# A two-layer decoder step on one Trainium2 core: the first loads are cut and reordered, and the last residual update is regrouped over three engines

## The reference, cut to what matters

```python
def trunk_layer(x, l, ...):
    h = rmsnorm(x, g_mix_pre[l])
    qa, ka, va, qi, ki, wi, qb, kb, vb, gb = project_mixers(h, w_in[l], pos)
    a = mixer_a(qa, ka, va, qi, ki, wi)            # indexer picks keys, sparse attention
    b, S = retention_mixer(qb, kb, vb, gb, s0, g_ret[l])
    x = x + rmsnorm(concat(a, b) @ w_out[l], g_mix_post[l])
    f = jnp.square(jax.nn.relu(rmsnorm(x, g_ffn_pre[l]) @ w_up[l])) @ w_down[l]
    return x + rmsnorm(f, g_ffn_post[l])

def rmsnorm(x, g):
    return x * lax.rsqrt(jnp.mean(x * x, axis=-1) + EPS) * g
```

## Time and profile before

| | us |
|---|---|
| median of 3 runs (1651.63 to 1654.96) | 1653.7 |
| the profiled execution, its own time | 1654.42 |
| its span, first to last instruction | 1652.6 |
| TensorE busy | 1580.8 |
| VectorE busy | 831.6 |
| ScalarE busy | 432.5 |
| GpSimd busy | 420.8 |

### The profile page before, as it was taken

The page is one execution under the profiler, slowest core; times in us unless marked ns, Lnnn a source line. Parts: engine busy times, 40 slices in busy tenths (PEclk is TensorE's granted clock), DMA queues, the critical chain, the costliest instruction groups (busy, mean ns, idle before and its releaser), DMA issues.

```text
span 1652.6 us, 19575 instructions
## 1 busy us (share of the span) xinstructions
PE 1580.8 (96%) x6986; PEld 1101.5 (67%) x6986; DVE 831.6 (50%) x1761; ACT 432.5 (26%) x975; POOL 420.8 (25%) x332
## 2 busy tenths in 40 slices
PE   7999899999999999999989998999999999999995
PEld 4344344478888888888843433445888888888884
DVE  4498556684743002332566984577646420133335
ACT  4312244314422002210142212443244310032100
POOL 0000000113363433353420000010226433343451
PEclk9999999999999999999999999999999999999998
DMA  6135401121422122312123252101233312222211
GB/s 203 63 127 167 146 20 52 53 78 55 153 102 103 72 82 102 103 51 102 63 94 102 77 202 105 52 1 54 81 103 127 105 74 103 102 80 100 77 51 52
DMA packets 52498, 150.26 MB, mean 91 GB/s; under 512 B 8331, under 2 KB 29331, under 8 KB 39091
## 3 DMA queue, kind: packets, MB, share of 16 engines
q1 hardware_dynamic: 44770, 140.65, 24.3%
q10 hardware_dynamic: 7632, 8.36, 1.5%
HBM read 139.79 MB, written 9.02 MB: 90 GB/s over the span
## 4 chain that ended last, share of the span: by engine, by line
PE 76%; DVE 16%; ACT 3%; issue 2%; DMA 2%; SPq 1%; ACTq 0%; DVEq 0%; POOL 0%; POOLq 0%
PE ps L1028 42%; PE ps L690 17%; PE ps L966 7%; DVE arena L1604 1%; DVE x_feat L1753 1%; DVE top L1602 1%; DVE arena L1643 1%; PE ps L694 1%; PE ps L828 1%; ACT arena L1182 1%; DVE s_sb L1751 1%; PE ps L815 1%; PE ps L838 1%; PE ps L649 1%; PE ps L924 1%
## 5 line engine op out<-in xcount | busy, mean ns | idle before, releaser
L690 PE MATMUL ps<-wring,h_feat 128*128 128x512 f32 (+1 forms) x960 | 438.6, 596 | 4.2 <-ACT arena L1182 2.8
L690 PEld LDWEIGHTS ps<-wring,h_feat 128*128 128x128 f32 x960 | 173.3, 193 | 192.7 <-issue 181.2
L1028 PE MATMUL ps<-arena,wring 128*128 128x256 f32 (+1 forms) x1280 | 285.8, 382 | 0.3 <-DVE arena L1832 0.3
L1028 PEld LDWEIGHTS ps<-arena,wring 128*128 128x128 f32 x1280 | 243.1, 190 | 37.7 <-DVE arena L1832 1.1
L1028 PE MATMUL ps<-h_feat,wring 128*128 128x256 f32 (+1 forms) x768 | 176.8, 382 | 2.5 <-DVE arena L1832 2.5
L2086 POOL TENSOR_TENSOR wring<-wring,arena 128x512 f32<-128x512 f32 (+1 forms) x48 | 78.8, 1641 | 341.2 <-PE ps L1028 321.6
L1028 PEld LDWEIGHTS ps<-h_feat,wring 128*128 128x128 f32 x768 | 145.8, 190 | 24.8 <-DVE arena L1832 3.3
L1028 PE MATMUL ps<-mix,wring 128*128 128x256 f32 (+1 forms) x512 | 123.6, 391 | 3.9 <-DVE s_sb L1806 3.9
L1028 PE MATMUL ps<-arena 128*128 128x264 f32 x512 | 119.2, 386 | 0.0
L966 PE MATMUL ps<-mix,wring 128*128 128x256 f32 (+1 forms) x512 | 115.0, 383 | 0.8 <-ACT mix L1242 0.8
L1028 PEld LDWEIGHTS ps<-mix,wring 128*128 128x128 f32 x512 | 99.4, 194 | 20.9 <-DVE s_sb L1806 4.8
(11 more groups left out here) (212 smaller groups left out, 1800.8 us busy)
## 6 DMA issues: line engine op xcount, KB each, us to landing
wring<-in_w_all SPq DMA_DIRECT2D x108, 1024.0 KB, 5.0
arena<-in_cache_k SPq DMA_DIRECT2D x32, 256.0 KB, 5.3
arena<-in_cache_v SPq DMA_DIRECT2D x32, 256.0 KB, 4.3
wring<-in_w_idx SPq DMA_DIRECT2D x4, 648.0 KB, 5.6
x_feat<-in_x SPq DMA_DIRECT2D x4, 520.0 KB, 6.4
o_k_out<-arena ACTq DMA_DIRECT2D x2, 1024.0 KB
o_v_out<-arena ACTq DMA_DIRECT2D x2, 1024.0 KB
arena<-in_state SPq DMA_DIRECT2D x2, 1024.0 KB, 4.9
```

Source lines behind the costliest of these rows:

```text
L690: last = mm(ps[:, proj_bank(n), 0:width], h_feat[:, k, token_cols(t)], wt, start=(k == 0), stop=(k == KD - 1))
L1028: last = mm(out, a[:, j, :], b, start=(opens(n) and j == 0), stop=(j == nk - 1), skip_group_check=True)
```

## The change

The x loads now come in pieces of 1, 1, 2, 2, 2 chunks and the first weights in pieces of 1, 1, 2, 4 chunks, issued alternately; `pg` comes after them. The squares of half 1, k = 4 and 6, in the last norm of both layers, are written by ScalarE to free slots of `p1s`; GpSimd no longer adds them, and TensorE multiplies them by the same matrix as `ssum`, into the same bank. In layer 1, for half 1, VectorE makes only the scaled product, in place in `osb`, with no wait between; TensorE has copied `x_feat` into eight banks by a product with the identity, adds the scaled `osb` by another, and ScalarE copies each bank to `x_feat`. The store of half 1 is cut into 4, 2 and 2 chunks.

```diff
+X_CUTS = (0, 1, 2, 4, 6, 8)
+W_CUTS = (0, 1, 2, 4, 8)
...
+def square_direct(norm, h, k):
+    return (norm, h) == (4, 1) and k in (4, 6)
...
+        def y_bank(k):
+            return ps[:, [n for n in range(8) if n != stat_bank(4)][k] if k < KD - 1 else stat_bank(4), 0:span(1)]
+        def direct_square(k):
+            return p1_at(LAST - 3 + (k == 6))
...
+            for n in range(len(X_CUTS) - 1):
+                k = slice(X_CUTS[n], X_CUTS[n + 1])
+                sp.dma_start(x_feat[:, k, :], x[:, k, :]).then_inc(x_in[n], 16)
+                if n < len(W_CUTS) - 1:
+                    u, cols = W_CUTS[n] // 4, slice(W_CUTS[n] % 4 * W_IDX, (W_CUTS[n] % 4 + W_CUTS[n + 1] - W_CUTS[n]) * W_IDX)
+                    sp.dma_start(wring[u][:, cols], w_idx[0, u, :, cols]).then_inc(first_w[n], 16)
             sp.dma_start(pg[:], pages).then_inc(pages_in, 16)
-            for k in range(0, KD, 2):
-                sp.dma_start(x_feat[:, k:k + 2, :], x[:, k:k + 2, :]).then_inc(x_in[k // 2], 16)
-                if k in (0, 4):
-                    u = k // 4
-                    sp.dma_start(wring[u][:, 0:4 * W_IDX], w_idx[0, u]).then_inc(first_w[u], 16)
...
-            for h in range(2):
-                for k in range(0, KD, 4):
-                    sp.wait_ge(x_ready, past(x_ready) + 2 * KD + h * KD + k + 4)
-                    sp.dma_start(y[:, k:k + 4, HALVES[h]], x_feat[:, k:k + 4, HALVES[h]]).then_inc(y_out, 16)
...
+            for k0, k1 in ((0, 4), (4, 6), (6, KD)):
+                sp.wait_ge(y_read, k1)
+                sp.dma_start(y[:, k0:k1, HALVES[1]], x_feat[:, k0:k1, HALVES[1]]).then_inc(y_out, 16)
...
-                mm(ps[:, stat_bank(4), 0:span(1)], ones[:], ssum[:, HALVES[1]], start=True, stop=True).then_inc(stat_mm, 1)
+                bank = ps[:, stat_bank(4), 0:span(1)]
+                mm(bank, ones[:], ssum[:, HALVES[1]], start=True, stop=False)
+                for k in (4, 6):
+                    pe.wait_ge(sq_ready, layer * PER_LAYER["sq_ready"] + square_number(layer, 4, 1, k)[0])
+                    last = mm(bank, ones[:], direct_square(k), start=False, stop=(k == 6))
+                last.then_inc(stat_mm, 1)
...
                     last_stats(l)
+                    pe.wait_ge(c12_ready, past(c12_ready) + LAST + 1)
+                    for k in range(KD):
+                        if k == KD - 1:
+                            pe.wait_ge(std_ready, counts[stat_mm.num])
+                        mm(y_bank(k), idn[:], x_feat[:, k, HALVES[1]], start=True, stop=False)
+                    for k in range(KD):
+                        pe.wait_ge(last_upd, k + 1)
+                        mm(y_bank(k), idn[:], osb[:, k, HALVES[1]], start=False, stop=True).then_inc(y_mm, 1)
...
                     deviation(4, 1)
+                    for k in range(KD):
+                        act.wait_ge(y_mm, k + 1)
+                        nc.scalar.activation(x_feat[:, k, HALVES[1]], y_bank(k), ACT.Copy).then_inc(y_read, 1)
...
-                for k in range(KD):
+                for k in range(KD if l == DEPTH - 1 else 0):
+                    o = osb[:, k, HALVES[1]]
+                    v.scalar_tensor_tensor(o, o, gcol[:, 2, k:k + 1], rstd_post[:, HALVES[1]], ALU.mult, ALU.mult).then_inc(last_upd, 1)
+                for k in range(KD if l < DEPTH - 1 else 0):
                     update(2, 1, k)
...
+                if square_direct(norm, h, k):
+                    return
```

More of the change, by code:

```diff
@@ L88, in head_steps, with cut_of @@
     return [(k, done(n, k)) for k in range(KD) if done(n, k + 1) > done(n, k)]
+def cut_of(cuts, k):
+    return max(n for n, c in enumerate(cuts[:-1]) if c <= k)
 def product_items():
@@ L205 @@
     c12_ready=24, ft_ready=64, c11_dve=4, dn_ready=16, knew_done=8, gain_ready=5, osq_ready=5,
-    pads_ready=1, sq_used=56, s_ready=96, kidx_in=256, gains_in=32, state_in=16, out_ki=32, out_k=32, out_v=32,
+    pads_ready=1, sq_used=54, s_ready=96, kidx_in=256, gains_in=32, state_in=16, out_ki=32, out_k=32, out_v=32,
     out_r=48, bounce=64, bounce_o=16, w_slot0=208, w_slot1=208, w_slot2=224, w_slot3=224, c_slot0=128, c_slot1=128,
@@ L226, in square_number @@
     n = order.index((norm, h, k)) + 1
-    return n, sum(1 for s in order[0:n] if not square_first(*s))
+    return n, sum(1 for s in order[0:n] if not square_first(*s) and not square_direct(*s))
 def counter():
@@ L354, in build @@
         const_in = sem("const_in"); zeroed = sem("zeroed"); y_out = sem("y_out")
-        x_in = [sem(f"x_in{i}") for i in range(KD // 2)]
+        x_in = [sem(f"x_in{i}") for i in range(len(X_CUTS) - 1)]
         gfirst_in = sem("gfirst_in")
-        first_w = [sem(f"first_w{i}") for i in range(2)]
+        first_w = [sem(f"first_w{i}") for i in range(len(W_CUTS) - 1)]
         pages_in = sem("pages_in")
@@ L365, in build @@
         state_in = sem("state_in")
+        last_upd = sem("last_upd")
+        y_mm = sem("y_mm")
+        y_read = sem("y_read")
         sq_ready = sem("sq_ready")
@@ L604, in _ @@
                     unit(u)
-            for h in range(2):
-                for k in range(0, KD, 4):
-                    sp.wait_ge(x_ready, past(x_ready) + 2 * KD + h * KD + k + 4)
-                    sp.dma_start(y[:, k:k + 4, HALVES[h]], x_feat[:, k:k + 4, HALVES[h]]).then_inc(y_out, 16)
-            sp.wait_ge(y_out, 64)
+            for k in range(0, KD, 4):
+                sp.wait_ge(x_ready, past(x_ready) + 2 * KD + k + 4)
+                sp.dma_start(y[:, k:k + 4, HALVES[0]], x_feat[:, k:k + 4, HALVES[0]]).then_inc(y_out, 16)
+            for k0, k1 in ((0, 4), (4, 6), (6, KD)):
+                sp.wait_ge(y_read, k1)
+                sp.dma_start(y[:, k0:k1, HALVES[1]], x_feat[:, k0:k1, HALVES[1]]).then_inc(y_out, 16)
+            sp.wait_ge(y_out, 80)
         @block.tensor
@@ L631, in last_stats @@
             def last_stats(layer):
-                pe.wait_ge(sq_used, layer * PER_LAYER["sq_used"] + max(square_number(layer, 4, 1, k)[1] for k in range(KD)))
+                pe.wait_ge(sq_used, layer * PER_LAYER["sq_used"] + max(square_number(layer, 4, 1, k)[1] for k in range(KD) if not square_direct(4, 1, k)))
                 pe.wait_ge(std_ready, counts[stat_mm.num])
-                mm(ps[:, stat_bank(4), 0:span(1)], ones[:], ssum[:, HALVES[1]], start=True, stop=True).then_inc(stat_mm, 1)
+                bank = ps[:, stat_bank(4), 0:span(1)]
[4 more added lines that the diff above has]
+                last.then_inc(stat_mm, 1)
                 up(stat_mm)
@@ L653, in first_chunk @@
                 for k in range(KD):
-                    if k % 4 == 0:
-                        pe.wait_ge(first_w[k // 4], 16)
+                    if k in W_CUTS:
+                        pe.wait_ge(first_w[cut_of(W_CUTS, k)], 16)
                     pe.wait_ge(first_h, k + 1)
@@ L1087, in _ @@
             for k in range(KD):
-                act.wait_ge(x_in[k // 2], 16)
+                act.wait_ge(x_in[cut_of(X_CUTS, k)], 16)
                 nc.scalar.activation(h_feat[:, k, :], x_feat[:, k, :], ACT.Copy, scale=gfirst[:, k:k + 1]).then_inc(first_h, 1)
@@ L1109, in square @@
                     dst = ssum[:, HALVES[h]]
+                elif square_direct(norm, h, k):
+                    dst = direct_square(k)
                 else:
@@ L2041, in _ @@
                 inverse(1, rstd_post)
-                for k in range(KD):
+                for k in range(KD if l == DEPTH - 1 else 0):
+                    o = osb[:, k, HALVES[1]]
+                    v.scalar_tensor_tensor(o, o, gcol[:, 2, k:k + 1], rstd_post[:, HALVES[1]], ALU.mult, ALU.mult).then_inc(last_upd, 1)
+                for k in range(KD if l < DEPTH - 1 else 0):
                     update(2, 1, k)
-                    if k == 2 and l < DEPTH - 1:
+                    if k == 2:
                         now[0] = l + 1
```

## The result

The changed kernel took 1639.61 us (median of 4 executions, 1635.28 to 1641.46), against 1652.66 for the kernel before, run beside it (4 executions, 1651.55 to 1654.96). The ratio on record is 0.9915, 95% interval 0.9892 to 0.9939 (the two medians alone give 0.9921): faster, by about 13 us or 0.8%. The profiled execution took 1641.46, the longest of its four, with a span of 1639.7 against 1652.6. So profile against profile the change is worth 12.9 us, where the prediction had 11.4.

A forecast was written before the change was run, and what follows sets the result against it. TensorE carries 76% of the chain, VectorE 16%, so gains come only where TensorE stands still. Start 6.5, end of layer 0 0.1, end 4.8 sum to 11.4: 1654.42 to 1643.0, less 0.7 gives 1642.3 us; range 1640.0 to 1647.0.

The forecast's parts named there:

- the end of layer 0: Where layer 0 ends: two additions leave GpSimd, VectorE gains 1.0 us, more products cost 0.9; net 0.1 gained.
- the base: Whole kernel: profiled execution 1654.42 us, with the median of the runs shown 0.7 lower.
- First loads: At the start: smaller pieces let TensorE start at 4.8 us instead of 6.85 and end the first projection at 26.0.
- the start term: Start to second projection: first bank taken 6.1 to 6.9 us earlier, counted as 6.5; second projection at 28.5.
- the bound of 7.0: At the start: the gain cannot pass 31.31 - 24.3 = 7.0 us, since TensorE's first bank is complete at 24.3.
- Constants: At the start: `pg` last holds the weight units until 21.3 us, so the last constant lands at 21.8 to 22.9.
- `wring2` too late: At the second projection: each us these weights land after 28.5 costs one; a loss at 39.9, 26.5 expected; chance 0.02.
- the whole rest moves forward together: After the start: all later loads wait on work done, so everything shifts equally, with 0 gained in layer 0's body.
- the middle loses: Rival, end of layer 0: remaining GpSimd additions slide under other VectorE instructions, products cost 0.9 us; time 1643.3; chance 0.08.
- Statistics at the end: At the end: the last statistics product starts 1.5 us earlier without GpSimd's wait, plus 0.4 less; gain 1.9.
- The last update and the store: At the end: TensorE sets the pace, last copy ends at 1644.8 us instead of 1649.19, store at 1647.8; 2.9 gained.
- The clock rival: Last 10 us: TensorE's clock at half; time 1649.6 us with all records slow, 1646.0 with half; chance 0.15.

The follow-up runs named there:

- r_after_again: The changed kernel run again unedited (also called the repetition): 1638.51 us, ratio 0.9915 to the kernel before.
- e1: The kernel before with only the new start (first loads in cut pieces, `pg` behind them), nothing at the end: 1644.61 us, ratio 0.9955.
- e2: The kernel before with only `pg` moved behind the first loads, whose pieces stay uncut: 1646.41 us, ratio 0.9961.
- e3: The kernel before with only the first loads cut as in the change, `pg` still issued first: 1652.64 us, ratio 1.0005.
- e8_direct_only: The kernel before with only the two direct squares (k = 4 and 6), in both layers: 1648.03 us, ratio 0.9977.
- e5_no_direct: The changed kernel without the direct squares, GpSimd adding k = 4 and 6 again in both layers: 1643.00 us, ratio 0.9945.
- e9: The kernel before with only the last update by TensorE and ScalarE and the store in 4, 2 and 2 tiles: 1650.95 us, ratio 0.9993.
- e10: The changed kernel without the direct squares, with six unused products put into TensorE's stop after the last layer product: 1641.87 us, ratio 0.9937.

## Why the prediction was right in its mechanisms and low by 1.5 us in its sum

The step that failed is the sum. Its term for the end of layer 0 was 0.1 and measured 0.8; the rest of layer 0 was put at nothing and measured 1.0; and the base it was taken from was about 1.1 too high. The mechanisms at the start and at the end came out as described. The ledger, profile against profile:

| stretch | predicted | measured |
|---|---|---|
| start to second projection | 6.5 | 6.1 |
| body of layer 0 | 0 | 1.0 |
| end of layer 0 | 0.1 | 0.8 |
| layer 1 | 0 | -0.1 |
| end | 4.8 | 5.1 |
| sum | 11.4 | 12.9 |

**First loads.** Right: first product at 4.91 for 4.8, first projection done at 26.75 for 26.0. "I let it run on without a gap" was so, but at 0.54 us a record for longer: the first 48 records take 16.38 in place of 15.77, and with the 0.1 at the start the first projection is done 0.7 later than expected. Of this 0.4 reach the second projection, by which the start term fell short. In the repetition the 48 take 15.06, and the start gains 7.4, more than the bound of 7.0, which took their pace as fixed.

**Constants.** Right. `pg` was expected in at 12.2 (the sum given for it makes 12.4) and the weight units at 21.3; they are issued at 20.72. The table load was put at 22 to 23 and is at 21.73, and e1 to e3 show that moving `pg` carries it. The feared side, `wring2` too late, does not show: the four records at 28.96 follow on ScalarE's copy.

**Body of layer 0.** This was taken as nothing ("the whole rest moves forward together"). Part of it is the landing of the cache tiles that TensorE waits for at about 145 us. The kernel before:

```profile
150.80 2.81 PE L797 MATMUL ps<-arena,qs 128*32 128x257 f32 x32 [2.43 <-DMA arena<-in_cache_k]
```

and the changed kernel:

```profile
143.21 1.95 PE L825 MATMUL ps<-arena,qs 128*32 128x257 f32 x32 [1.24 <-DMA arena<-in_cache_k]
```

1.19 less wait, and 0.86 less in the records, which ran partly at half clock before. The changed kernel pays part of that back from 174.03 on, where its clock falls. Another 0.3 comes right at the second projection, whose first records ran at half clock before (2.26) and take 1.95 now. This wait for the cache follows no edit: it is 1.77 in r_after_again and lies between 1.06 and 2.55 over all kernels. But the stretch as a whole, from the second projection to the end of layer 0, is shorter than the kernel before's by 1.0 to 3.9 us in all nine profiles with `pg` last (1.0 here, 2.6 in r_after_again) and by 0.0 to 0.6 in the three others with `pg` first. So "moves forward together" was too simple. How much of it the edit brings and how much is chance, one profile for each kernel does not settle: the same kernel ran from 1634.31 to 1641.46.

**End of layer 0: the step that was mis-sized.** Its bounds held (1.0 gained, 0.9 lost), its value did not. Two slow VectorE instructions, at 820.02 and 825.07, were counted as those that the removed additions cause. There were four in the stretch; 821.89 (1.04) and 822.96 (0.95) ran beside GpSimd additions that stay. With two additions gone, the others fall elsewhere (`814.67 1.63 POOL L2115`, two in a row), and only one slow instruction (0.84) is left. The rival "the middle loses" thought of that sliding with the wrong sign. Measured: 1.7 gained on VectorE, 0.89 paid for the products, 0.8 net.

**Statistics at the end.** 1.9 predicted, 1.9 in e8_direct_only. The three products stand as described: two ahead, the third 0.06 after its square. The 0.4 counted for the clock is near the 0.5 by which e3's tail is shorter.

**The last update and the store.** 2.9 predicted, 3.1 measured. VectorE's eight instructions run at 3.32 / 8 = 0.415 each, below the bound of 0.43, and TensorE sets the end of the stretch, as said. The last copy ends 9.8 us after the last layer product where 10.3 were expected: the first pass starts 0.1 sooner, and the second follows it with none of the 0.2 of fill. From the last copy to the end it is 3.2, against 3.0.

**The clock rival.** It was refuted for the changed kernel (1.00 to the end of TensorE's work) and shown for a neighbour: take the direct squares out and the first pass runs at half clock. The reason given ("the fall only after a real stop") holds as far as it goes: no fall after 0.63 here, a fall in the stop of 3.00 in e5_no_direct, but none in that of e3. The Trainium skill's page "TensorE: Matmul & The Clock Gate", section "A second HAM failure mode: psum-queue depth-cycling", cited for that rival, was not put to the test: it speaks of idle gaps from bank to bank, and the second pass shows none (its 16 records take 3.72, as the first pass's do), though the program waits eight times.

**The base and the range.** The forecast of 1642.3 lies 2.7 above the measured median. 1.5 of this is the ledger. The other 1.1 is the base: the profiled execution was put 0.7 above the median, on three executions; four give 1652.66, 1.8 below the profiled one, and the changed kernel's profiled execution lies 1.85 above its own median. Later 25 executions of the kernel before had a median of 1652.06 (1648.21 to 1657.4); from there the same sum gives 1640.7, and with the 0.7 of layer 0's end 1640.0. And the lower end, 1640.0, was made of the bounds of the start, the middle and the store (0.5 + 0.9 + 0.4 = 1.8, down to 1640.5), which leaves 0.5 us for the spread, while single executions of the changed kernel lie 7 us apart. That the median came out 0.4 below the range, and not inside it, is within this spread.

## What to carry to other kernels

When a load is late, look at what the loads ahead of it release: here the page table, once last, held back megabytes of weights and let 13 small constants through, and cutting the first pieces paid only after that. Before work is given to TensorE at the end of a program, take away the stop ahead of it: after a stop of 3 us the clock was at half in five of six kernels here. The two edits together were worth 5.1 where apart they gave 1.9 and 0.6 to 2.1. Do not read a difference of 1 us between two single profiles as the edit's before the same kernel has been profiled twice: here its start alone moved by 1.3. Build the range from the spread of executions as well as from the costs: three runs did not fix the base to better than 1.6 us.

## What the runs showed of the hardware

- With a stop of TensorE of 3.0 us at the end, the granted clock fell to 0.50 in before, e1, e2, e5 and e9 and stayed at 1.00 in e3; with waits of 0.42 and 0.63 there (e10, after) it did not fall. After equal stops the same 16 records took 6.23 in one kernel and 4.78 in the other.
- At the start TensorE's records are 0.54 us apart and then 0.27, although the granted clock is shown as 1.00. The change comes 3.4 us after the first record in r_after_again, 6.1 in after; this moves the start by up to 1.3 us.
- Every kernel with `pg` first (before, e3, e8, e9) has a stretch at half clock that begins between 29.9 and 32.3 us, in TensorE's wait for banks or at its end; none with `pg` last has one there. The first four records of the second projection take 1.95 at full clock, 2.26 in before and 3.75 in e8.
- VectorE's two-input instructions of 256 or 264 columns take 0.42 to 0.49 alone and 0.84 to 1.05 when they start while a GpSimd addition runs. One that was already running when the addition began kept its 0.48 (before, 819.51), and one that reads PSUM took 0.43 wholly beside an addition (after, 815.75). Eight with no wait between them took 0.415 each.
- Most of ScalarE's issues of the constants take 0.45 each while SyncE issues nothing (after), and 0.46 to 0.72 while SyncE issues cache tiles (before, e3, e9).
